# A two-layer decoder trunk: one more add in the search, exponentials behind a high side, first one-hots ahead of the last add, and the last gate of a layer unsummed

## What is computed

```
h    = rmsnorm(x);  proj = h @ w_in           # q, k, v, pool, gMLP and six half-width gates
g    = sigmoid(proj_gates + b_gate)
x   += (g0 * attention @ wa + g1 * pool @ wb + g2 * gmlp @ wc) @ w_out
h2   = rmsnorm(x)
s1, s2 = scores of 8 heads against 128 + 128 sub-keys; top 16 of each;
top 16 of the 16 x 16 sums; softmax -> gate, idx = i1 * 128 + i2
x   += sum_k gate_k * gelu(h2 . expert_u[idx_k]) * expert_v[idx_k]
```

## Time and profile before

| | |
|---|---|
| median of 3 runs | 2027.26 us (2025.8 to 2027.57) |
| the profiled execution's own time | 2030.79 us |
| its span, first to last instruction | 2028.9 us |
| mean granted TensorE clock | 0.998 |
| TensorE busy | 2003.4 us, 99% |
| VectorE busy | 1534.6 us, 76% |
| ScalarE busy | 1054.6 us, 52% |
| GpSimd busy | 1030.9 us, 51% |

### The profile page before, as it was taken

How to read it: one execution, slowest core, us unless ns; L and a number is a source line. 1 busy time by engine, 2 the same in 40 slices (tenths; PEclk the granted TensorE clock), 3 DMA queues, 4 the chain that set the end, 5 groups by cost and what they waited for, 6 DMA issues and landing times.

```text
span 2028.9 us, 39016 instructions
## 1 busy us (share of the span) xinstructions
PE 2003.4 (99%) x12276; PEld 1793.8 (88%) x12276; DVE 1534.6 (76%) x3160; ACT 1054.6 (52%) x1730; POOL 1030.9 (51%) x425
## 2 busy tenths in 40 slices
PE   9999999999999999999999999999999999999998
PEld 7998788899999888888889988888999998888887
DVE  1866369988887888888638653799888878888886
ACT  5644455567776333333466444555677753333333
POOL 6799779787775000000268898797777740000001
PEclk9999999999999999999999999999999999999999
DMA  8455557676665777777774555576656668777875
GB/s 247 134 195 186 177 185 234 211 229 197 196 196 194 245 241 241 241 240 241 238 218 136 187 182 198 196 236 211 217 197 198 195 206 244 242 240 242 241 243 174
DMA packets 172124, 429.56 MB, mean 212 GB/s; under 512 B 19156, under 2 KB 83957, under 8 KB 171510
## 3 DMA queue, kind: packets, MB, share of 16 engines
q1 hardware_dynamic: 171588, 425.56, 66.1%
q10 hardware_dynamic: 434, 2.63, 0.3%
HBM read 392.79 MB, written 35.32 MB: 211 GB/s over the span
## 4 chain that ended last, share of the span: by engine, by line
PE 76%; POOL 10%; issue 8%; DVE 3%; ACT 1%; DMA 1%; POOLq 0%; DVEq 0%; ACTq 0%; SPq 0%
PE bank L1599 33%; PE bank L1321 20%; POOL halves L547 10%; PE bank L1585 9%; PE bank L1587 5%; PE bank L1650 3%; PE bank L1343 3%; PE bank L1345 1%; DMA ring<-in_stream 1%; PE bank L1565 1%; DVE area L1176 0%; DVE area L1180 0%; DVE area L1183 0%; DVE area L933 0%; ACT halves L628 0%
## 5 line engine op out<-in xcount | busy, mean ns | idle before, releaser
L547 POOL TENSOR_TENSOR halves<-ring,halves 128x1024 fp32r<-128x1024 f32 x412 | 1025.3, 2502 | 976.6 <-DVE coef L1264 682.9
L628 ACT ACTIVATE halves<-ring 128x1024 fp32r<-128x1024 f32 x668 | 704.9, 1056 | 707.0 <-PE bank L1599 412.4
L1599 PE MATMUL bank<-halves,coef 128*128 128x512 f32 x3000 | 681.4, 389 | 0.0
L1599 PEld LDWEIGHTS bank<-halves,coef 128*128 128x128 f32 x3000 | 562.6, 188 | 117.5 <-issue 0.5
L1321 PE MATMUL bank<-hT,halves 128*128 128x256 f32 x4512 | 565.7, 283 | 0.2
L1321 PEld LDWEIGHTS bank<-hT,halves 128*128 128x128 f32 x4512 | 552.2, 192 | 2.2 <-issue 0.7
L1244 DVE TENSOR_TENSOR halves<-ring,halves 128x1024 fp32r<-128x1024 f32 x256 | 315.6, 1233 | 10.2 <-ACT halves L628 10.2
L1585 PE MATMUL bank<-hT,halves 128*128 128x512 f32 x896 | 311.4, 393 | 3.1 <-POOL halves L547 3.1
L1587 PE MATMUL bank<-hT,halves 128*128 128x256 f32 x896 | 249.5, 279 | 0.0
L1585 PEld LDWEIGHTS bank<-hT,halves 128*128 128x128 f32 x896 | 167.8, 187 | 41.3 <-issue 3.7
L1343 PE MATMUL bank<-hT,halves 128*128 128x512 f32 x512 | 181.3, 399 | 1.7 <-DVE hT L922 1.7
(11 more groups left out here) (174 smaller groups left out, 1704.7 us busy)
## 6 DMA issues: line engine op xcount, KB each, us to landing
ring<-in_stream SPq DMA_DIRECT2D x668, 512.0 KB, 3.9
held_blocks<-act SPq DMA_DIRECT2D x244, 128.0 KB, 1.8
act<-held_blocks SPq DMA_DIRECT2D x244, 128.0 KB, 3.0
area<-rel_scratch SPq DMA_DIRECT2D x16, 128.0 KB, 6.3
area<-in_gains SPq DMA_DIRECT2D x4, 512.0 KB, 4.8
x_home<-x ACTq DMA_DIRECT2D x2, 1024.0 KB, 3.9
x<-x_home SPq DMA_DIRECT2D x2, 1024.0 KB, 8.1
area<-in_params SPq DMA_DIRECT2D x2, 640.0 KB, 7.7
```

Source lines behind the costliest of these rows:

```text
L547: pool.tensor_tensor(halves[:, s, 1, :], ring[:, s, :], halves[:, s, 0, :].bitcast(F32), ALU.subtract)\
L628: a.activation(halves[:, s, 0, :], ring[:, s, :], ACT.Copy).then_inc(hi_done, 1)
L1599: i = pe.matmul(acc[2 * t + hf][:, :], coef[:, k, a, t * P:(t + 1) * P], halves[:, s, e, hf * HALF_N:(hf + 1) * HALF_N], start=opens and n ...
```

## The change

Four edits. (1) `fold()` once more in the search, behind the bitwise_and of the ranks; VectorE then stops the adds in front of the weights one earlier than before (`PARKED - 1` in the last loop). (2) ScalarE's exponentials come behind the high side of turn 44 and ahead of its gelu; the eight turns from there are written out instead of looped. (3) The last add comes behind the first one-hots, and ScalarE scales these ahead of its last turn; TensorE waits for the last add before the first table product. (4) Gate 5, the last of a layer, is plain and no longer summed.

```diff
-PLAIN = 2
+SUMMED = (2, 3, 4)
+PLAIN = (0, 1, 5)
...
-    + [step for kind, n in MIX[1:] for step in (... [("gate", "A")] * 2 if n < PLAIN else [("sum", "V")] * 4)]
+    + [step for kind, n in MIX[1:] for step in (... [("gate", "A")] * 2 if n not in SUMMED else [("sum", "V")] * 4)]
...
+                        if n not in SUMMED and n >= 3 and k == 0:
+                            a.wait_ge(taken_v, l * NGV + taken_before(place("branch", 2 * (n - 2) + 1) + 1)[0])
...
                 with a.Fori(0, EXP_AT) as r:
                     for s in range(RING):
                         turn(r, s)
-                a.wait_ge(shifted_ready, l + 1)
-                a.activation(sel[:, 2], sel[:, 2], ACT.Exp).then_inc(gexp_ready, 1)
-                a.activation(stat[:, 13:14], one, ACT.Gelu_apprx_tanh)
-                with a.Fori(EXP_AT, PARKED // RING - 1) as r:
+                for r in range(EXP_AT, PARKED // RING - 1):
                     for s in range(RING):
-                        turn(r, s)
+                        if r == EXP_AT and s == 0:
+                            a.wait_ge(tiles_used, l * NT + r * RING + (T_PU + s + 1))
+                            high(r * RING + (T_PU + RING + s), s)
+                            a.wait_ge(shifted_ready, l + 1)
+                            a.activation(sel[:, 2], sel[:, 2], ACT.Exp).then_inc(gexp_ready, 1)
+                            a.activation(stat[:, 13:14], one, ACT.Gelu_apprx_tanh)
+                            park(r, s)
+                        else:
+                            turn(r, s)
...
+                    if s == RING - 1:
+                        weighted(0)
                     turn(PARKED // RING - 1, s)
...
-                a.wait_ge(weights_hi, 2 * l + 2)
-                weighted(0)
                 for n in range(SETS):
+                    if n == 1:
+                        a.wait_ge(act_done, l * NK + PARKED)
...
                 link(v.tensor_scalar(cb..., 15, None, ALU.bitwise_and))
+                fold()
...
-                while folds[0] < PARKED:
+                while folds[0] < PARKED - 1:
                     fold()
...
                 onehots(0)
+                fold()
                 onehots(1)
...
                     pe.wait_ge(onehots_ready, l * SETS + n + 1)
+                    if n == 0:
+                        pe.wait_ge(sides_added, (l + 1) * PARKED)
```

More of the change, by code:

```diff
@@ L117 @@
     + [("pT0", "A")] * 2 + [("pT1", "A")] * 4 + [("attn", "A")] * 4 + [("gmlp", "V")] * 2 + [("pool", "V")] * 2
-    + [step for kind, n in MIX[1:] for step in ([("branch", "V")] * 2 if kind == "branch" else [("gate", "A")] * 2 if n < PLAIN else [("sum", "V")] * 4)]
+    + [step for kind, n in MIX[1:] for step in ([("branch", "V")] * 2 if kind == "branch" else [("gate", "A")] * 2 if n not in SUMMED else [("sum", "V")] * 4)]
     + [("wo", "V")] * 3 + [("h2T", "V")] * 2 + [("wo", "V")] + [("h2T", "V")] * 2 + [("qq", "V")] * 2 * PH + [("score", "A")] * 8
@@ L718, in gates @@
                         high_up_to(T_GATE[n] + 2 * k + 1 + 3)
-                        if n < PLAIN:
+                        if n not in SUMMED and n >= 3 and k == 0:
+                            a.wait_ge(taken_v, l * NGV + taken_before(place("branch", 2 * (n - 2) + 1) + 1)[0])
+                        if n not in SUMMED:
                             b = group("gate")
@@ L724, in gates @@
                             into = sig_of(n)[:, 2 * k + c, :]
[L725 to L728, removed]
+                            if n in SUMMED:
+                                a.wait_ge(taken_v, l * NGV + taken_before(place("sum", 4 * (n - SUMMED[0]) + 2 * k + c) + 1)[0])
+                            i = a.activation(into, b[:, c * S:(c + 1) * S] if n not in SUMMED else into, ACT.Sigmoid, bias=par[:, col:col + 1])
+                        i.then_inc(sig_done, 1) if n in SUMMED else i.then_inc(taken_a, 1)
                 gates(0)
@@ L785, in turn, with weighted @@
                     park(r, s)
+                def weighted(n):
+                    a.wait_ge(low_placed, l * SETS + n + 1)
+                    for u in range(2, FOUR):
+                        rows = onehot2[:, n % 2, u, 0, :]
+                        i = a.activation(rows, rows.bitcast(F32), ACT.Copy, scale=weight[:, n, u - 2:u - 1])
+                    i.then_inc(onehots_ready, 1)
                 with a.Fori(0, EXP_AT) as r:
@@ L811, in hold @@
                     gelu(i % 2)
[L813 to L820, removed]
                 def side(q):
@@ L1042, in _ @@
                     for br in range(BR):
-                        if PLAIN <= 3 * hf + br + 1 < 2 * BR:
+                        if 3 * hf + br + 1 in SUMMED:
                             add_gates(3 * hf + br + 1)
@@ L1049, in _ @@
                             s = sig_of(3 * hf + br)[:, 2 * n:2 * n + 2, :]
-                            if 3 * hf + br < PLAIN:
-                                v.wait_ge(taken_a, l * NGA + taken_before(place("gate", 2 * (3 * hf + br) + n) + 1)[1])
+                            if 3 * hf + br not in SUMMED:
+                                v.wait_ge(taken_a, l * NGA + taken_before(place("gate", 2 * PLAIN.index(3 * hf + br) + n) + 1)[1])
                             else:
-                                v.wait_ge(sig_done, l * 2 * (2 * BR - PLAIN) + 2 * (3 * hf + br - PLAIN) + n + 1)
+                                v.wait_ge(sig_done, l * 2 * len(SUMMED) + 2 * SUMMED.index(3 * hf + br) + n + 1)
                             if br == 0:
@@ L1184, in _ @@
                         fold()
+                assert EXP_AT * RING < folds[0] <= PARKED - 2, folds[0]
                 v.wait_ge(gexp_ready, l + 1)
```

## The result

The changed kernel takes 2038.18 us (median of 4 runs, 2037.14 to 2039.53); the kernel before, on the same chip, takes 2026.53 us (2025.04 to 2027.57). The ratio is 1.0053, with a 95% interval from 1.004 to 1.0065: slower by 11.7 us. Run again later on one chip with other kernels, it gave 1.0056 (1.0043 to 1.0069). The profiled execution went from 2030.79 to 2039.53 us, its span from 2028.9 to 2037.7.

What follows compares the result with a forecast made beforehand. TensorE, busy 99%, was taken as the bound. Per layer +3.45 (projection) +0.6 (search) -1.1 (one-hots) = +2.95, both layers +5.9, clock +3.2: +9.1 us on the median 2027.26 gives 2036.4 us, range 2031.0 to 2042.5.

Steps and rivals of the forecast that it cites:

- The banks: Output projection: TensorE waits for its PSUM banks until VectorE takes branch 5's last group; starts 3.75 us later a layer.
- the plain gate: Gate 5's four tiles on TensorE: three-matmul form instead of summed form, +0.2 us a layer.
- The circle in the argument: Late projection leaves GpSimd idle, so VectorE's subtraction for branch 5 takes 0.70 us instead of 2.77.
- The search: End of the search: the extra add lengthens VectorE's chain, so the key transposes start 0.6 us later a layer.
- the wait of 1.5 us: TensorE's wait for GpSimd's low sides at L1585: goes, but is not won, as TensorE then waits for the keys.
- The wait for the keys: TensorE's wait in front of the key transposes (L1624): grows from 0.65 to about 3.0 us.
- The one-hots: First one-hots ahead of the last add: TensorE's wait in front of the first table product goes, -1.1 us a layer.
- The clock: TensorE's clock falls to 1.2 GHz behind two of four long waits, 1.58 us each, +3.2 us; bounds 0 and 6.3.
- The rule of the Trainium skill: Idle gaps between TensorE's matmul bursts bring the slow clock: falls at all four waits, +6.3 us, 2039.5; rival's chance 0.14.

Runs made afterwards that it cites:

- the gate alone: Only gate 5 made plain instead of summed, on the kernel before: 2037.29 us, 1.0051.
- with other banks: Kernel before with gate 5 plain, output projection's PSUM banks moved to 4 to 7, those of the transposed rows to 0 to 3: 2025.91 us, 0.9997.
- the short idle matmuls: Changed kernel with 7 and 6 throwaway matmuls in its two long TensorE waits, ahead of the projection's banks and the keys: 2033.24 us, 1.0029.
- the gate summed: Changed kernel with gate 5 summed again, so only the first three edits on the kernel before: 2025.98 us, 1.0005.
- the add alone: Kernel before with only the first edit, one more add behind the bitwise_and: 2032.13 us, 1.0015.
- the exponentials alone: Kernel before with only the second edit, exponentials behind the high side of turn 44 and eight turns written out: 2027.85 us, 1.0003.
- all four with other banks: Changed kernel, all four edits, with the projection's banks at 4 to 7 and the transposed rows' at 0 to 3: 2028.88 us, 1.001.
- the later transposes without the add: Kernel before with the second and third edits and the key transposes one parked block later, gate 5 summed, no extra add: 2027.39 us, 0.9997.

## Why the prediction was right

The forecast was 2036.4 us in a range of 2031.0 to 2042.5, and the kernel took 2038.18; +9.1 us were forecast on the median and +11.7 came.

**The banks.** Right in place and mechanism: the gate alone loses 0.51% (some 0.2% of it by the other cause), with other banks nothing, and other banks give the changed kernel 8.7 us back. Right in size: +3.75 was forecast with 0.2 for the plain gate; the trace has 3.32 more between branch 5's last matmul and the projection's first (3.44 against 0.12), and 0.2 for the plain gate (11.52 us for its four tiles against 11.32). That it is so close is partly luck: the forecast left out the 0.36 us from the end of VectorE's take to TensorE's start, and it let the cast end when it ended before, where it ended 0.47 us earlier against the start of branch 5 (7.39 against 7.86). The circle in the argument held: the late projection stops GpSimd, which frees VectorE's subtraction (0.69 us), which shortens the wait. Without it the wait would have been some 2 us longer, an estimate from the 2.81 us of the subtraction with other banks against 0.69. The projection itself became 0.4 us shorter at equal clock (22.6 and 24.1 us with the short idle matmuls, 22.97 and 24.49 with the gate summed), as forecast.

**The search.** +0.6 was forecast for the transposes, +0.47 came, and 0.14 of the difference is the normalisation, which took 0.60 where it took 0.74 before. That the wait of 1.5 us would not be won but move to the keys is shown twice, by the add alone and by the exponentials alone. The wait for the keys was forecast at 3.0 and is 2.9.

**The one-hots.** -1.1 forecast; from block 54 to the table it was 9.56 us before and 8.50 with the three edits at full clock: -1.06.

**The clock.** This term was mis-sized. I took two falls in four waits, +3.2 us. In the profiled execution the clock fell behind all four: the projections lost 1.45 and 2.7 us (24.06 and 26.88 against 22.6 and 24.1; the higher base of layer 1 goes with VectorE's normalisation, whose two instructions took 3.6 us there beside GpSimd and 1.4 in layer 0), the blocks behind the transposes 1.57 twice (10.07 against 8.50), 7.3 us together. One fall costs about what the earlier trace rows said, 1.58; in layer 1's projection the slow stretch was twice as long. In the second profiled execution of the changed kernel the clock fell behind all four too, once each, and by the same reckoning that cost 6.2 us. Taken over all profiled kernels with such waits (the changed kernel twice, the gate alone, the three edits, all four with other banks, the add alone), the clock fell behind 5 of 6 waits of 3.16 us and behind 6 of 10 of 2.9 us; it fell behind none of the four waits of 1.8 to 2.4 us (the exponentials alone, the later transposes without the add). In the queries, where no single wait is over 1.3 us, it fell in 4 of 28 layers. So two in four was too low for the changed kernel, and "all" holds for its two profiled executions but not for every kernel with such waits. The rule of the Trainium skill (TensorE: Matmul & The Clock Gate, "Why this matters for your kernels"), taken as a fall at all four, gives 4 x 1.58 = 6.3 and 2039.5, which is 1.3 us too high where my two falls are 1.8 us too low; the time does not decide between them, the two traces are on the side of the rule.

**What the spans show.** The profiled spans differ by 8.8 us only, because the execution before had a fall in the queries of layer 0 (1.6 us) and VectorE's normalisation stretched beside GpSimd there (L933, 2.96 us for one instruction; 1.5 us more for the projection); after, neither happened in layer 0, and 3.1 us came back. I take that for chance and not for the change, because each is there in some executions of the other kernels and missing in others; with the change, the normalisation of layer 0 was short in one profiled execution and long in the other. The terms for both layers are 6.6 + 0.4 - 0.8 + 0.9 - 2.1 = +5.0 without the clock. For the profiled execution, 5.0 + 7.3 - 3.1 gives 9.2 against the 8.8 of the spans. The changed kernel with short idle matmuls, where the clock did not fall, measured 5.9 above the kernel before (1.0029).

**What was luck.** The forecast had 5.9 without the clock, and 5.0 came; it had 3.2 for the clock, and 6 to 7 came in the profiled executions. The two errors have opposite signs and partly cancel in the time.

## What to carry to other kernels

When a list hands out banks in turn and a later user has fixed banks, taking two entries out of the list changes who is last in those banks; count the last users again after every such edit. An extra piece of work in a chain is free only on an engine that waits; here the chain of the search set the end, so that the wait removed ahead of it came back behind it. Two things gave time: the first one-hots ahead of the last add, and, on top of the first three edits, asking for the chain's result one block later; the second did so with the extra add and not without it. On a TensorE that is 99% busy a new wait of 3 us costs more than it lasts, because the clock may fall behind it; a few idle matmuls that end ahead of the release gave that part back here, and twice as many cost 6 us.

## What I had not expected

The parked blocks ran at another pace in the kernel with the gate alone, at full clock and with the same instructions: 39 blocks took 110.33 us in both layers, against 108.25 before and in all other kernels. Windows of TensorE in that kernel, then in the kernel before:

```profile
272.76:383.09 110.33, 110.33 (x628) 1.00 0.68 221
1281.60:1391.92 110.32, 110.32 (x627) 1.00 0.67 221
```
```profile
270.99:379.24 108.25, 108.25 (x628) 1.00 0.70 225
```

That is 0.053 us a block, spread over its matmuls and not one wait, and 2.1 us a layer. At the 48th block GpSimd was less late (a wait of 1.0 us instead of 1.5), but the blocks up to there had lost as much more, so that the transposes came 154.50 us behind the first parked block, before 152.45: 2.05 us a layer, some 4 of the 10 to 11 us that this kernel loses. With the banks swapped (the next run) the stretch took 108.25 again. What sets the pace was not tried and stays open.
